# Dilated attention on one core: the dilated attention's queries and keys projected by halves of the heads, the second half beside the first half's attention

## What is computed

```python
def _dilated_attention(h, w_in, q_norm, k_norm, w_out):
    qkv = (h @ w_in).reshape(b, s, 3, 3, 8, 64)      # q/k/v, 3 groups, 8 heads, 64
    q = _rmsnorm(qkv[:, :, 0], q_norm)
    k = _rmsnorm(qkv[:, :, 1], k_norm)
    v = qkv[:, :, 2]
    ...
    # per group: causal scores at distances that are multiples of the group's dilation,
    # minus slope * distance, softmax; one softmax over the three groups of a head
    ...
    o = jnp.sum(wts[..., None] * o_all, axis=0) / jnp.sum(wts, axis=0)[..., None]
    return o.astype(h.dtype).reshape(b, s, DIL_OUT_WIDTH) @ w_out
```

## Time and profile before

| | us |
|---|---|
| median of 3 runs | 2123.14 |
| lowest and highest | 2115.45, 2125.70 |
| the profiled execution, whole | 2121.36 |
| its span | 2119.6 |

### The profile page before, as it was taken

One profiled execution on the slowest core, in us unless ns is written; L12 is line 12 of the kernel. 1 busy time (PEld: TensorE's weight loads), 2 busy tenths in 40 slices (PEclk: granted clock), 3 DMA queues, 4 the chain that ended last, 5 costly groups with the idle time before them and its releaser, 6 DMA issues.

```text
span 2119.6 us, 29100 instructions
## 1 busy us (share of the span) xinstructions
PE 1907.0 (90%) x12247; PEld 1643.4 (78%) x12247; DVE 1127.6 (53%) x1577; ACT 904.9 (43%) x1394; POOL 336.2 (16%) x390
## 2 busy tenths in 40 slices
PE   5889878999999998968899968898899999999999
PEld 2766657888877887846799858888799978768997
DVE  2455557555574544574455536753455455565554
ACT  3444344344555343633444435333344444434443
POOL 2020231211231222120111110031200005200000
PEclk9999888999999999988999969998999999989999
DMA  8454554454656675320656523310255555504554
GB/s 274 139 201 139 166 171 141 156 173 148 210 176 199 204 237 191 122 77 20 198 179 187 172 90 120 120 60 1 85 165 183 174 171 174 187 1 134 184 181 138
DMA packets 217966, 320.61 MB, mean 151 GB/s; under 512 B 8550, under 2 KB 123946, under 8 KB 217452
## 3 DMA queue, kind: packets, MB, share of 16 engines
q1 hardware_dynamic: 212628, 308.96, 45.1%
q0 software_dynamic: 1744, 6.03, 0.8%
q10 hardware_dynamic: 3464, 3.75, 0.5%
HBM read 317.68 MB, written 1.05 MB: 150 GB/s over the span
## 4 chain that ended last, share of the span: by engine, by line
PE 74%; DVE 12%; ACT 6%; DMA 4%; POOL 2%; issue 2%; SPq 0%; POOLq 0%; ACTq 0%; DVEq 0%
PE ps L69 71%; DVE WLO L86 3%; PE ps L77 3%; DVE AR L96 2%; ACT WHI L80 1%; DVE AR L86 1%; DMA RAW<-in_w_up_dram 1%; DMA RAW<-in_w_mod_dram 1%; ACT AR L80 1%; DMA RAW<-in_w_in_dram 1%; POOL SM L86 1%; DVE SM L99 1%; ACT XR L80 1%; POOL XR L86 1%; ACT PMD L80 1%
## 5 line engine op out<-in xcount | busy, mean ns | idle before, releaser
L86 DVE TENSOR_TENSOR WLO<-RAW,WHI 128x1024 fp32r<-128x1024 f32 (+3 forms) x506 | 592.5, 1213 | 430.8 <-ACT WHI L80 430.6
L80 ACT ACTIVATE WHI<-RAW 128x1024 fp32r<-128x1024 f32 (+3 forms) x506 | 488.2, 1014 | 398.0 <-PE ps L69 287.6
L69 PE MATMUL ps<-TH,WHI 128*128 128x256 f32 x1664 | 483.2, 290 | 28.8 <-DVE WLO L86 18.2
L69 PE MATMUL ps<-TL,WHI 128*128 128x256 f32 x1664 | 477.8, 287 | 0.0
L69 PE MATMUL ps<-TH,WLO 128*128 128x256 f32 x1664 | 477.3, 287 | 0.0
L69 PE MATMUL ps<-WHI,ARR 128*128 128x512 f32 x1120 | 354.5, 393 | 5.5 <-DVE ARR L86 3.1
L69 PEld LDWEIGHTS ps<-TH,WHI 128*128 128x128 f32 x1664 | 326.5, 196 | 39.9 <-issue 24.9
L69 PEld LDWEIGHTS ps<-TL,WHI 128*128 128x128 f32 x1664 | 327.2, 197 | 0.2
L69 PEld LDWEIGHTS ps<-TH,WLO 128*128 128x128 f32 x1664 | 326.4, 196 | 0.0
L69 PE MATMUL ps<-WHI,TH 128*128 128x512 f32 (+3 forms) x624 | 246.7, 395 | 24.0 <-DVE WLO L86 23.0
L69 PEld LDWEIGHTS ps<-WHI,ARR 128*128 128x128 f32 x1120 | 210.2, 188 | 56.5 <-issue 9.3
(11 more groups left out here) (180 smaller groups left out, 1930.1 us busy)
## 6 DMA issues: line engine op xcount, KB each, us to landing
RAW<-in_w_mod_dram SPq DMA_DIRECT2D x48, 1024.0 KB, 5.5
RAW<-in_w_up_dram SPq DMA_DIRECT2D x48, 1024.0 KB, 5.5
RAW<-in_w_down_dram SPq DMA_DIRECT2D x48, 1024.0 KB, 5.2
RAW<-in_ffn_w_in_dram SPq DMA_DIRECT2D x44, 1024.0 KB, 5.1
RAW<-in_w_in_dram SPq DMA_DIRECT2D x20, 1024.0 KB, 5.3
RAW<-in_ffn_w_out_dram SPq DMA_DIRECT2D x20, 1024.0 KB, 5.1
RAW<-in_dil_w_in_dram SPq DMA_DIRECT2D x18, 1024.0 KB, 5.1
RAW<-in_gdn_w_in_dram SPq DMA_DIRECT2D x16, 1024.0 KB, 5.6
```

The costliest lines, as they stand in the source:

```text
L69: return Made(None if self.eng is None else self.eng.matmul(o, l, r, start=start, stop=stop))
L80: return Made(None if self.eng is None else self.eng.activation(o, i, f, **k))
L86: return Made(None if self.eng is None else self.eng.tensor_tensor(o, a, b, op))
```

## The change

The six query and key pieces are regrouped: a piece now holds 256 columns (4 heads) of each of two of the six (kind, group) pairs, so three pieces give all queries and keys of heads 0 to 3 and three more those of heads 4 to 7. Each of their weight tiles is loaded with two DMAs of 512 KB in place of one of 1 MB. The projection's generator takes a half: half 0 is three query/key pieces and the three value pieces (24 steps), half 1 the other three pieces (12 steps and `LAG` more). `dil_order` runs half 0, then weaves half 1 (15 items) with the first 8 steps of the attention (units of heads 0 to 3), then runs the other 11 steps. The scores of a unit wait for their half only. In the woven part the sums use banks 0, 1, 2, the projection's transposes bank 3, the attention banks 5, 6, 7 (and 4 as before); afterwards the attention has seven banks again. The ScalarE copy after the transposes and the GpSimd gain are two instructions of 256 columns each in place of one of 512. The logits move to free space in AR, and the output of the attention gets a place of its own (DOH, DOL), since the projection's input is still in use.

```diff
@@ -347,6 +347,12 @@
+                elif t.name == "dil_w_in_2" and t.c0 < 3072:
+                    for i, (kind, g) in enumerate(DQKS[t.c0 // 512][1:]):
+                        c0 = 1536 * kind + 512 * g + 256 * DQKS[t.c0 // 512][0]
+                        sp.dma(t.of(t.raw)[:, :, 256 * i:256 * i + 256],
+                               T[t.name][t.idx][128 * t.k0:128 * (t.k0 + t.nk), c0:c0 + 256].rearrange("(k p) n -> p k n", p=128)).then_inc(
+                                   w_land[t.i % NRAW], t.i)
...
@@ -2837,31 +2843,34 @@
-        LG = [X2[0][:, 768 * i:768 * i + 768] for i in range(2)]
+        LG = [AR[:, 13568 + 768 * i:14336 + 768 * i] for i in range(2)]
+        DOH, DOL = [x[:, 2048:3072].rearrange("p (k t) -> p k t", k=4) for x in (TH, TL)]
         DI = PMD[:, 0:1536].rearrange("p (t g n) -> p t g n", t=2, g=3)
-        DQKS = [(g, kind) for g in range(3) for kind in range(2)]
-        DSTEPS = [("qk", x, c, ti) for x in range(6) for c in range(2) for ti in TLS]
-        DSTEPS += [("v", g, c, ti) for g in range(3) for c in range(2) for ti in TLS]
+
+        DPIECES = [(kind, g) for kind in range(2) for g in range(3)]
+        DQKS = [(half, *DPIECES[2 * j:2 * j + 2]) for half in range(2) for j in range(3)]
+        DHALF = [[("qk", x, c, ti) for x in range(3 * half, 3 * half + 3) for c in range(2) for ti in TLS] for half in range(2)]
+        DHALF[0] += [("v", g, c, ti) for g in range(3) for c in range(2) for ti in TLS]
 
         def d_spec(kind, x):
-            c0 = 1536 * DQKS[x][1] + 512 * DQKS[x][0] if kind == "qk" else 3072 + 512 * x
-            return spec("dil_w_in_2", 0, 0, 8, c0, 512)
-
-        def d_given(s):
-            return DSTEPS[s] if 0 <= s < len(DSTEPS) and DSTEPS[s][2] == 1 else None
+            return spec("dil_w_in_2", 0, 0, 8, 512 * x if kind == "qk" else 3072 + 512 * x, 512)
+
+        def d_given(steps, s):
+            return steps[s] if 0 <= s < len(steps) and steps[s][2] == 1 else None
 
         def nrm_of(x, ti):
             i = 2 * x + ti - 2
             return NRM[i % 4], ((x - 2, ti) if x >= 2 else None), s_pj[i % 4]
 
-        def pe_dproject():
-            for s in range(len(DSTEPS) + LAG):
-                if s < len(DSTEPS):
-                    kind, x, c, ti = DSTEPS[s]
+        def pe_dproject(half):
+            steps = DHALF[half]
+            for s in range(len(steps) + LAG):
+                if s < len(steps):
+                    kind, x, c, ti = steps[s]
                     if c == 0 and ti == 2:
                         g = pe_rows(("d" + kind, x), d_spec(kind, x), TLS, rows_of("dil"), normed("dil"))
                     next(g)
-                if (r := d_given(s - LAG)) and r[0] == "qk":
+                if (r := d_given(steps, s - LAG)) and r[0] == "qk":
                     x, ti = r[1], r[3]
...
+                yield
+
+        def act_dproject(half):
             act.wait_ge(pe_gemm, ("acc", (("fd", 0), 1), 3))
...
-                    g, kind = DQKS[x]
                     act.wait_ge(pe_pj, ("dturn", x, ti))
-                    dst = (KTd if kind else QTd)[:, 4 * g:4 * g + 4, 128 * ti - 256:128 * ti - 128]
-                    act.act(dst, h4(banks.of(("dt", x, ti))), ACT.Copy, scale=1.0 if kind else 0.125).then_inc(
-                        act_pj, ("free", ("dt", x, ti)), "dqk")
-
-        def pool_dproject():
-            for s in range(len(DSTEPS)):
-                kind, x, c, ti = DSTEPS[s]
-                if c == 1 and kind == "qk":
+                    b4 = h4(banks.of(("dt", x, ti)))
+                    for i, (kind, g) in enumerate(DQKS[x][1:]):
+                        k0 = 4 * g + 2 * half
+                        m = act.act((KTd if kind else QTd)[:, k0:k0 + 2, 128 * ti - 256:128 * ti - 128], b4[:, 2 * i:2 * i + 2, :], ACT.Copy,
+                                    scale=1.0 if kind else 0.125)
+                    m.then_inc(act_pj, ("free", ("dt", x, ti)), ("dqk", half))
+                yield
...
-                    pool.tt(n3, n3, mid(DQK[:, DQKS[x][1], :], 8), ALU.mult).then_inc(pool_pj, ("drow", x, ti))
-
-        def dve_dproject():
+                    for i, (kind, g) in enumerate(DQKS[x][1:]):
+                        m = pool.tt(n3[:, 4 * i:4 * i + 4], n3[:, 4 * i:4 * i + 4], mid(DQK[:, kind, :], 4), ALU.mult)
+                    m.then_inc(pool_pj, ("drow", x, ti))
...
@@ -2943,10 +2965,10 @@
-                    b1, b2 = [banks.take(("ds", j, step), ring) for j in range(2)]
+                    b1, b2 = [banks.take(("ds", j, step), aring) for j in range(2)]
                     wait_free(("ds", 0, step))
                     wait_free(("ds", 1, step))
-                    pe.wait_ge(act_pj, "dqk")
+                    pe.wait_ge(act_pj, ("dqk", h // 4))
...
-                        b = banks.take(key, ring)
+                        b = banks.take(key, aring)
...
+                yield
...
                     act.wait_ge(pe_at, ("do", u))
-                    act.wait_ge(pe_gemm, ("acc", ("dv", 2), 3))
-                    act.act(OH[:, c, :], banks.of(("do", c))[:, 0:256], ACT.Copy).then_inc(act_at, ("doh", c))
+                    act.act(DOH[:, c, :], banks.of(("do", c))[:, 0:256], ACT.Copy).then_inc(act_at, ("doh", c))
+                yield
...
-                    dve.tt(OL[:, c, :], banks.of(("do", c))[:, 0:256], OH[:, c, :].bitcast(F32), ALU.subtract).then_inc(
+                    dve.tt(DOL[:, c, :], banks.of(("do", c))[:, 0:256], DOH[:, c, :].bitcast(F32), ALU.subtract).then_inc(
                         dve_at, ("free", ("do", c)), ("dol", c))
+                yield
+
+        def dil_rows(k, ti):
+            cs = slice(128 * ti - 256, 128 * ti - 128)
+            return DOH[:, k, cs], DOL[:, k, cs]
...
+        def dil_order(project, attention):
+
+            run(project(0))
+            yield
+            at = attention()
+            weave((project(1), 12 + LAG), (part(at, 8), 8))
+            yield
+            run(at)
...
-            pe_dproject()
-            ring.set(0, 1, 2, 3, 5, 6, 7)
-            pe_dattention()
+            order = dil_order(pe_dproject, pe_dattention)
+            next(order)
+            gring.set(0, 1, 2)
+            ring.set(3)
+            aring.set(5, 6, 7)
+            next(order)
+            aring.set(5, 6, 7, 0, 1, 2, 3)
+            run(order)
+            gring.set(0, 1, 2, 3)
             ring.set(4, 5, 6)
-            pe_out("do", DIL_OUT, rows_of("dil"), dil_need, "ffn1")
+            pe_out("do", DIL_OUT, dil_rows, dil_need, "ffn1")
...
-            act_dproject()
-            act_dattention()
+            run(dil_order(act_dproject, act_dattention))
...
-            pool_dproject()
+            run(dil_order(pool_dproject, nothing))
```

More of the change, by code:

```diff
@@ L2872, in pe_dproject @@
                     m.then_inc(pe_pj, ("dturn", x, ti))
-        def act_dproject():
+                yield
+        def act_dproject(half):
             act.wait_ge(pe_gemm, ("acc", (("fd", 0), 1), 3))
-            for s in range(len(DSTEPS) + LAG):
-                if s < len(DSTEPS):
-                    kind, x, c, ti = DSTEPS[s]
+            steps = DHALF[half]
+            for s in range(len(steps) + LAG):
+                if s < len(steps):
+                    kind, x, c, ti = steps[s]
                     if ti == 2:
@@ L2891, in act_dproject, with pool_dproject @@
                             act_pj, ("free", (("dv", x), ti)), ("dv", x))
-                if (r := d_given(s - LAG)) and r[0] == "qk":
+                if (r := d_given(steps, s - LAG)) and r[0] == "qk":
                     x, ti = r[1], r[3]
-                    g, kind = DQKS[x]
                     act.wait_ge(pe_pj, ("dturn", x, ti))
-                    dst = (KTd if kind else QTd)[:, 4 * g:4 * g + 4, 128 * ti - 256:128 * ti - 128]
-                    act.act(dst, h4(banks.of(("dt", x, ti))), ACT.Copy, scale=1.0 if kind else 0.125).then_inc(
-                        act_pj, ("free", ("dt", x, ti)), "dqk")
-        def pool_dproject():
-            for s in range(len(DSTEPS)):
-                kind, x, c, ti = DSTEPS[s]
-                if c == 1 and kind == "qk":
+                    b4 = h4(banks.of(("dt", x, ti)))
[5 more added lines that the diff above has]
+                yield
+        def pool_dproject(half):
+            steps = DHALF[half]
+            for s in range(len(steps) + LAG):
+                if (r := d_given(steps, s)) and r[0] == "qk":
+                    x, ti = r[1], r[3]
                     sv = nrm_of(x, ti)[2]
@@ L2908, in pool_dproject @@
                     pool.tt(sv, sv, NH[:, 0:8], ALU.pow).then_inc(pool_pj, ("drstd", x, ti))
-                if (r := d_given(s - 1)) and r[0] == "qk":
+                if (r := d_given(steps, s - 1)) and r[0] == "qk":
                     x, ti = r[1], r[3]
@@ L2912, in pool_dproject @@
                     pool.wait_ge(dve_pj, ("dnorm", x, ti))
```

(30 more changed lines are left out.)

## The result

| | us |
|---|---|
| median before, 20 runs | 2122.92 |
| median of the changed kernel, 20 runs | 2126.29 (2122.87 to 2130.62) |
| ratio | 1.0022, 95% interval 1.0013 to 1.0031 |
| profiled execution: whole, span | 2129.09, 2127.3 |

The change makes the kernel slower by 0.2%, 3.4 us, which is under the 0.5% that I had called no change. The forecast was 2124.5, with 2115.5 to 2135 as its range.

What follows compares the result with a forecast made beforehand. TensorE was taken to bound the projection, leaving only the attention's idle and half-clock time to win: -9.0 us won, +8.5 stalls, +2.0 clock, sum +1.5, so 2122.9 us as profiled and 2124.5 for the median, range 2115.5 to 2135.

Steps and rivals of the forecast that it cites:

- The ceiling, 9.0 us: First eight attention steps: 27.28 us before less 18.24 of work, the most that hiding them can give.
- S0: Attention, TensorE: scores of the first unit of a pair, put at 0.83 us.
- T0: Attention, TensorE: transposes for the first unit of a pair, put at 0.41 us.
- The new stalls, 8.5 us: Woven part: TensorE waits of 0.8, 1.9, 0.4, 3.0, 0.4 and 2.0 us, set against the 9.0 won.
- a3: Woven attention step 3: TensorE waits 1.9 us for a bank until VectorE has taken the scores.
- p13: Woven projection item 13: TensorE stands 3.0 us for GpSimd's gain, done about 5.6 us after item 11 ends.
- The clock, +2.0: Behind the gap at projection item 13: a likely clock fall, taken as short, 4 us at half speed, costing 2 us.
- long case: Clock fall behind the gap at projection item 13: 12.7 us at half clock, costing 5.3 us.
- Rival 1: Woven part: overlap holds, bank waits vanish, tail 3 us, clock stays; -4 to -6 us; chance 0.15.
- Rival 2: Woven part: clock falls twice, at attention step 3 and the tail; about +11 us, 2134; chance 0.13.
- Rival 3: Projection: the halved weight loads become the bound; +16 us, 2140; chance 0.02.
- Rival 5: Woven part, ScalarE: table loads as exponentials and Squares alternate; +3 to +5 on the sum, 2127 to 2130; chance 0.02.

Runs made afterwards that it cites:

- the two profiles: The changed kernel's first profile, and one from timing it again unchanged on another occasion; ratio 1.0022 at first, 1.0016 the second time.
- the filled gap in the kernel before: The kernel before with three useless products in the gap of 2.69 us at the start of the attention; 0.9982, stage 159.6 us.
- the kernel with the first gap filled: The changed kernel with useless products only ahead of the last but one turn, none ahead of unit 8; 0.9997, stage 164.9 us.
- both gaps filled: The changed kernel with useless TensorE products in both gaps at the end of the woven part; 1.0012, stage 163.8 us.
- the kernel with the swap: The changed kernel with GpSimd's gain of the last but one block ahead of the last block's mean and root; 0.9982, stage 162.2 us.
- four banks and the same order of work: The changed kernel with four banks for the attention and two for the projection's sums in the woven part; 1.0049, stage 172.9 us.
- the regrouping alone: The changed kernel without weaving: regrouped queries and keys, then values, then the whole attention; 0.9997, stage 164.9 us.
- weaving the pieces that need one copy: The kernel before with its last 8 value steps woven with the first three attention steps, no regrouping; 0.9973 and 0.9971.
- attention steps ahead: The changed kernel with attention steps 5 and 6 ahead of the last two turns, step 7 behind them; 1.0031, stage 168.2 us.
- two banks for the sums: Two kernels with four attention banks: the changed kernel's order, 1.0049, and attention steps 5 and 6 ahead of the last turns, 1.0066.

## Why the prediction came out as it did

The sign and the mechanism held: the gap at the end of the woven part stood where it was put, ended by GpSimd's gain, and the clock fell behind it. The size was short. The sum said +1.5, the medians say +3.4 and +5.0, and the stages of the two profiles +7.1 and +4.0. That the median lies only 1.8 us above the forecast is partly luck: the clock's term was far too small, and the stalls came out right only because two errors in them cancel. (2122.9 and the 1.8 of the profiled execution make 2124.7, not the 2124.5 that I wrote.)

*The ceiling, 9.0 us.* Right as a difference of what was measured, but it mixed two things that behave differently: 5.1 of half clock and 3.9 of idle time, as the filled gap in the kernel before shows. The work in it was read a little short: in the changed kernel S0 takes 0.86 us (1864.49 to 1865.35) and T0 0.48 (1865.35 to 1865.83), where I had 0.83 and 0.41. That is 0.3 us over the eight steps, so the ceiling is about 8.7.

*The new stalls, 8.5 us.* I had put 0.8 at p5: it isn't there. At a3 1.9: it was 1.18. At a5 and a7 0.4 each: 0.26 and, at half clock, none. At p13 3.0: 2.41, at T + 5.3 where I had said T + 5.6, and GpSimd's gain behind the root, as named. Ahead of unit 8 2.0: 0.84 at half clock, 1.67 at full clock in the kernel with the first gap filled. That is about 5.5 in gaps and not 8.5. The woven part nevertheless took 64.0 us in place of 62, since some 6 us of its end ran at half clock, about 3 us lost, and since each change between the two streams costs a little, for which my sum had no term: with both gaps filled it takes 63.4, 9.5 over the 53.9 of work, of which 4.6 are the filling and 2.1 are gaps. Of the other 2.8, 0.3 is the work read short; the rest I put down to these changes from stream to stream (some 15), as a remainder and not read one by one. So 3.0 too much in the gaps and 2.8 not counted make a sum that is right by luck. A smaller term, put at nothing, went the other way: behind the woven part the first pair of units has no waits and takes 5.86 us in the kernel with the swap, so the second part is 30.5 us at full clock and not 31.3. The pairs after it keep 6.72.

*The clock, +2.0.* This is the mis-sized term. The gap came, it was as long as those that had brought a fall, and the fall came; I took the short case with 4 us of half clock, and it was 24 and 17 us. In the second part alone it is 37.6 us against 31.3, +6.3, in the first profile, and +3.3 in the second. My reason for the short case was dense work on both sides; in fact there are no projection steps behind the gap any more, only a7, one turn and the attention. But that isn't shown to be the cause of the long fall either: with four banks and the same order of work the gap at this place is 2.88 us, and 3.4 us of half clock follow it. The long case in my sum, 5.3, taken from the gap before, would have given 2128.0 for the median, 1.7 too high.

*Added work, half 0, the loads.* Right: the regrouping alone is at 0.9997. Half 0 keeps its time: 1743.60 to 1813.59 is 70.0 us, and before it is 70.0 as well (105.9 for 36 steps, less 12 x 2.72 and six turns).

*The rivals.* Rival 1, the overlap holds, didn't come true as told in any kernel: with the swap the clock stays and the ratio is 0.18% under the kernel before, but the wait for a bank at a3 is still 1.18 us. Rival 2, two falls, didn't occur: 1.18 us at a3 brought none. One long fall cost, in the first profile, 6.3 us in the second part and about 3 in the woven part: more than the 5.3 of my long case, less than the 11 of this rival. Rival 3: loads of 512 KB landed in 4.2 us and ScalarE didn't wait for RAW. The trace before already spoke against my 8.1 of the earlier trace rows: it has tiles of 512 KB loaded by a single DMA too, which landed in 3.4 and 3.8 us. Rival 5: no table load shows between the Squares and the exponentials; in the changed kernel's timeline of ACT a single one stands from 1812 to 1880, ahead of the first exponential:

```profile
1815.78 1.28 ACT L80 ACT_TABLE_LOAD   x1
```

What stays open is why the half clock lasts 24 us in one execution and 17 in the next behind the same gap, and 3.4 in a kernel with a longer one. Between the two executions of the changed kernel the stage follows that length; what sets it, no run here tells.

## What to carry to other kernels

Count the end of a chain that used to be covered. Here three pieces of values lay behind the queries and keys and hid their path through four engines; weaving pieces whose results are needed at once took this cover away, while weaving the pieces that need one copy gave 6.7 us of the stage, the most of any kernel here, and with less code. Split an idle stretch into idle time and half clock before calling it a ceiling: filling a gap of 2.7 us with useless products was worth 0.18% by itself (0.06 to 0.31), and is a cheap way to measure it. Where two blocks share a slow engine near the end, look at which instruction stands first. And when a wait for a buffer is to be removed, look for the wait that takes its place: the fourth bank took away 1.2 us and brought waits of 2.1 to 3.4.

## What the runs showed of the hardware

VectorE's scaling of 128 x 768 SBUF operands, from the changed kernel's instructions by form between 1813 and 1872:

```profile
L92 DVE TENSOR_SCALAR AR<-AR,SM 128x768 f32<-128x768 f32 x3 | 3.4, 1117 | 0.1
L92 DVE TENSOR_SCALAR AR<-AR,SM 128x384 f32<-128x384 f32 x3 | 1.3, 420 | 0.1
```

In the kernel before the same instruction takes 620 ns in all eight cases, when GpSimd has nothing to do. The three slow ones here each lie beside GpSimd instructions (the last at 1867.94, GpSimd's gain at 1867.89); those of 128 x 384, which come when GpSimd is idle, keep 420. VectorE's reductions and additions beside GpSimd's gains kept their times. The gains took 1.72 to 1.76 us for two in these three places and 1.41 in the other three. That the two engines hinder each other here is an inference; no kernel was made for it, but two bear on it. With the swap the gain is nearly over (1865.13 to 1866.54) when the third scaling starts at 1866.33, and this takes 0.62 us. With attention steps ahead a scaling of 128 x 384 falls beside a gain (1844.01, the gain from 1843.30 to 1844.72) and takes 0.93 us.

The gaps of TensorE and what followed in the stage: 2.69 us, 13.6 us of half clock; 2.41 and 2.40, 24 and 17; 2.72, 17; 1.67, once 3.4 and once none; 0.94 and 1.18, none. With two banks for the sums: 2.89, 6.8; 3.07, 3.4; 2.88, 3.4; 2.07, 3.4; 3.39, 3.4; 2.12 with one of 1.63 close behind it, 13.6. So every gap of over 2 us in this stage had a fall behind it, and its length did not go with that of the gap.
